# Per-chunk tiles for the scan scores and the products within a chunk

## What is computed

```python
    q_dec = q * jnp.exp(cum)
    k_inv = k * jnp.exp(-cum)
    k_end = k * jnp.exp(tot - cum)
    lower = jnp.tril(jnp.ones((HG_CHUNK, HG_CHUNK), dtype=bool))
    att = jnp.where(lower, jnp.einsum('bcthk,bcshk->bchts', q_dec, k_inv), 0.0)
    o_intra = jnp.einsum('bchts,bcshv->bcthv', att, v)
    ds = jnp.einsum('bcshk,bcshv->bchkv', k_end, v)
    ...
    o_inter = jnp.einsum('bcthk,bchkv->bcthv', q_dec, jnp.moveaxis(s_prev, 0, 1))
    return (o_intra + o_inter).reshape(b, n, h, -1), s_fin
```

## Time and profile before

| | |
|---|---|
| Time, median of 3 runs | 3948.75 us (3945.76 to 3953.18) |
| The profiled execution: its time, its span | 3950.17 us, 3948.4 us |
| Busy in the span: PE, weight loads, DVE | 2936.2, 1318.3, 2782.2 us |
| Busy in the span: ACT, POOL | 676.8, 1314.6 us |
| Mean granted clock of TensorE | 0.875 of full speed |

### The profile page before, as it was taken

The page is one execution under the profiler, slowest core; times in us unless marked ns, Lnnn a source line. Parts: engine busy times, 40 slices in busy tenths (PEclk is TensorE's granted clock), DMA queues, the critical chain, the costliest instruction groups (busy, mean ns, idle before and its releaser), DMA issues.

```text
span 3948.4 us, 46329 instructions
## 1 busy us (share of the span) xinstructions
PE 2936.2 (74%) x16906; PEld 1318.3 (33%) x16906; DVE 2782.2 (70%) x6805; ACT 676.8 (17%) x1391; POOL 1314.6 (33%) x1174
## 2 busy tenths in 40 slices
PE   8999999988899997856666666656656666665555
PEld 3665665545444442212222222212212222221111
DVE  4545546766787786747888868877877886877555
ACT  2534533011122120000111110110111111101000
POOL 0000000013433443433444434444444444444443
PEclk9999999989999998978888778878877788887777
DMA  4010003579999999999999999999999999999998
GB/s 184 24 35 26 24 25 150 183 259 404 410 414 417 412 399 417 416 422 414 400 399 413 418 409 411 417 414 415 418 413 412 419 412 416 416 411 413 420 419 340
DMA packets 214904, 1346.40 MB, mean 341 GB/s; under 512 B 24818, under 2 KB 45810, under 8 KB 63762
## 3 DMA queue, kind: packets, MB, share of 16 engines
q0 software_dynamic: 165888, 1208.03, 74.4%
q1 hardware_dynamic: 47492, 132.79, 9.0%
q10 hardware_dynamic: 1296, 2.62, 0.2%
HBM read 1329.69 MB, written 13.67 MB: 340 GB/s over the span
## 4 chain that ended last, share of the span: by engine, by line
DMA 37%; PE 36%; DVE 13%; issue 10%; POOL 2%; ACT 1%; POOLq 0%; SPq 0%; DVEq 0%; ACTq 0%
DMA arena<-in_uv,mask_b 14%; PE ps L787 12%; DMA arena<-in_uv,mask_f 11%; DMA arena<-in_uv,ones 11%; PE ps L1465 10%; DVE arena L1306 4%; PE ps L652 3%; PE ps L765 3%; POOL arena L621 2%; DVE arena L1187 2%; PE ps L1459 2%; PE ps L683 1%; PE ps L716 1%; DVE arena L1147 1%; PE ps L1517 1%
## 5 line engine op out<-in xcount | busy, mean ns | idle before, releaser
L787 PE MATMUL ps<-arena 64*64 64x512 f32 x9216 | 1451.0, 756 | 952.6 <-DVE arena L1187 946.9
L1306 DVE CUSTOM_DVE_ANT_0 arena<-arena 128x1024 f32<-128x1024 f32 x1152 | 1411.1, 1225 | 740.7 <-DMA arena<-in_uv,mask_b 292.9
L787 PEld LDWEIGHTS ps<-arena 64*64 64x64 f32 x9216 | 349.8, 157 | 1896.4 <-DVE arena L1187 1389.2
L621 POOL DMA_INDIRECT arena<-in_uv,ones x384 | 440.7, 1148 | 622.6 <-PE ps L787 480.8
L621 POOL DMA_INDIRECT arena<-in_uv,mask_f x384 | 441.3, 1149 | 584.9 <-PE ps L787 495.6
L621 POOL DMA_INDIRECT arena<-in_uv,mask_b x384 | 426.9, 1112 | 593.4 <-PE ps L787 506.4
L982 ACT ACTIVATE arena<-arena 128x2 f32<-128x2 f32 x576 | 117.1, 203 | 2646.1 <-DVE arena L1306 2645.8
L1465 PE MATMUL ps<-arena 128*128 128x384 f32 x1152 | 384.3, 490 | 1.8 <-DVE arena L1752 1.8
L1187 DVE TENSOR_SCALAR arena<-arena 128x64 f32<-128x64 f32 x1152 | 307.9, 310 | 0.4 <-ACT arena L982 0.3
L765 PE MATMUL ps<-arena 128*128 128x384 f32 x768 | 268.3, 496 | 0.0
L603 POOL IOTA arena<- 128x16 f32 x1 | 0.1, 144 | 804.0 <-PE ps L665 804.0
(11 more groups left out here) (209 smaller groups left out, 2358.6 us busy)
## 6 DMA issues: line engine op xcount, KB each, us to landing
arena<-in_w_mg SPq DMA_DIRECT2D x16, 1536.0 KB, 21.4
arena<-in_w_in SPq DMA_DIRECT2D x28, 512.0 KB, 3.4
arena<-in_w_mod SPq DMA_DIRECT2D x8, 1792.0 KB
arena<-in_w_mod SPq DMA_DIRECT2D x4, 2048.0 KB, 23.4
arena<-in_w_out SPq DMA_DIRECT2D x2, 4096.0 KB, 16.9
arena<-in_w_q SPq DMA_DIRECT2D x8, 1024.0 KB, 16.2
arena<-in_w_q SPq DMA_DIRECT2D x4, 2048.0 KB, 35.9
arena<-x_scratch SPq DMA_DIRECT2D x15, 512.0 KB, 11.6
```

The costliest lines, as they stand in the source:

```text
L621: nc.gpsimd.indirect_dma_start(out=RG[n % RING], out_offset=None, in_=uv, in_offset=bass.IndirectOffsetOnAxis(ap=EIDX[t % 3][:, s:s + 1], ...
L787: mm = nc.tensor.matmul(PS[c * HALF:(c + 1) * HALF, 2 * r + n, :], DG[rows, s, :], RG[s][rows, D + n * 512:D + (n + 1) * 512], start=(g == ...
L1306: ins = v.tensor_tensor_reduce(u, u, h2, 1.0, 0.0, ALU.mult, ALU.add, PRE[:, s % RING:s % RING + 1])
```

## The change

In `scores`, the one matmul of scores becomes four, one for each chunk: 32 columns of weights and 32 moving columns, each into its own 32 rows of the same 32 columns of bank 2. The copy by ACT has 160 columns in place of 256, the masked copy by DVE 32 in place of 128, under a mask `mask_c` that eight small copies build at the start of the heads' part. In `outputs`, the one matmul within the chunks becomes four on the array's diagonal, 32 rows and 32 columns of weights, each with the 128 value columns of its own 32 rows.

```diff
+    mask_c = sb("mask_chunk", [P, 2, CHUNK])
...
                 nc.tensor.transpose(PS[:, 2, 0:P], KE[d][:, sl], ident[:])
-                nc.tensor.matmul(PS[:, 2, P:2 * P], KI[d][:, sl], QD[d][:, sl],
-                                 start=True, stop=True).then_inc(ket_r, 1)
+                for j in range(CPT):
+                    c = slice(tt * P + j * CHUNK, tt * P + (j + 1) * CHUNK)
+                    mm = nc.tensor.matmul(PS[j * CHUNK:(j + 1) * CHUNK, 2, P:P + CHUNK], KI[d][:, c], QD[d][:, c],
+                                          start=True, stop=True)
+                mm.then_inc(ket_r, 1)
...
-                nc.tensor.matmul(OUT, ATT[:, d, it % 2, :], Vt[:, tt, :], start=True, stop=False)
+                for j in range(CPT):
+                    own = slice(j * CHUNK, (j + 1) * CHUNK)
+                    nc.tensor.matmul(OUT[own], ATT[own, d, it % 2, 0:CHUNK], Vt[own, tt, :], start=True, stop=False)
...
-                A(KET[:, it % 2, :], PS[:, 2, 0:2 * P], ACT.Copy).then_inc(ket_e, 1)
+                A(KET[:, it % 2, 0:P + CHUNK], PS[:, 2, 0:P + CHUNK], ACT.Copy).then_inc(ket_e, 1)
...
         dve.wait_ge(s_c, 2)
+        for d, m in enumerate((mask_f, mask_b)):
+            for j in range(CPT):
+                own = slice(j * CHUNK, (j + 1) * CHUNK)
+                ins = v.tensor_copy(mask_c[own, d, :], m[own, own])
+        ch(ins)
 
         v.memset(ef[:], 0.0).then_inc(lru_done, 1)
...
-                v.copy_predicated(ATT[:, d, it % 2, :], (mask_f, mask_b)[d][:].bitcast(I32),
-                                  KET[:, it % 2, P:2 * P]).then_inc(att_m, 1)
+                v.copy_predicated(ATT[:, d, it % 2, 0:CHUNK], mask_c[:, d, :].bitcast(I32),
+                                  KET[:, it % 2, P:P + CHUNK]).then_inc(att_m, 1)
```

## The result

The changed kernel takes 3962.3 us (median, 3956.72 to 3965.11) against 3948.18 for the kernel before, both over 9 runs: ratio 1.0033, 95% interval 1.0025 to 1.0042. It is slower by 14 us, where 3961 was forecast. The profiled execution took 3962.74 us, its span is 3961.0 against 3948.4.

The account below looks back on a forecast made before the run. PE was taken to bound the head-by-head part, DMA the rest. Over four heads, 3.66 us lost in projection steps less 0.48 gained elsewhere gave +12.7 us, so 3961 us against the median 3948.75; range 3951 to 3971.

Parts of the forecast that it names:

- What bounds: Head-by-head part: PE is the bound, and what the scan gains or loses arrives at the end at full size.
- The price list: On PE: tile change 0.09 us, exposed load 0.11 (128 columns) or 0.03 (32), pass 0.11 or 0.03, four tiles 0.02.
- Scores in a projection step: Scores as four tiles in steps with a projection: 0.40 us for 0.22, +0.18, between +0.12 and +0.34.
- Products in a projection step: Products within a chunk as four 32*32 tiles, steps with a projection: 0.36 us for 0.22, +0.14.
- The lower bound: Products: change from 32*32 to 128*32 is free, +0.02 us a projection step, +4.1 in all, 3953; 12%.
- Gate steps: Steps 0 to 5 of each head: the outputs' products get cheaper, -0.06 us a step.
- What was costed at nothing: Narrower ACT and DVE copies and eight mask copies (at most 2.3 us): hidden, except ACT's copy ahead of step 0.
- Off the chain from step 1 on: ACT's copies: in the chain of waits only ahead of a head's step 0, where the shorter copy saves 0.08 us.
- The sum: Four heads, each 3.66 us lost in projection steps and 0.48 gained elsewhere: +12.7 us, 0.3% slower.
- Free changes around the new tiles: Rival: tile changes that no row shows cost nothing and loads run ahead; 10.4 us faster, 3938; 5%.
- Turns of the four diagonal tiles: Rival: the products' four 32*32 tiles run in turns, +0.66 us in all 72 steps, +47, about 4009; 3%.
- The clock: Rival: PE's granted clock falls to 1.2 GHz in the gate steps, 21 us more, about 3982; 4%.

Follow-up runs that it names:

- e1: Kernel before with only the products within a chunk as four 32*32 tiles, scores and both copies unchanged: 3952.57 us, ratio 1.0014.
- e2: Kernel before with only the scores as four 128*32 tiles, both copies at old width, products unchanged: 3955.1 us, ratio 1.0024.
- e4: Kernel before with 48 extra matmuls of 128*128 tile and 128 moving columns inside late projection halves: 3958.74 us, ratio 1.0031.
- e12: Kernel before with late scores behind the outputs' 128*32 tiles, DVE's second-mixer piece first, 32*32 products in gate steps only: 3943.34 us, ratio 0.9987.
- e5: Kernel before with scores of steps 7 to 17 as 128*32 tiles behind the previous step's outputs, DVE copying from bank 7: 3980.76 us, ratio 1.008.
- e3: Kernel before with 48 extra matmuls of 128*32 tile and 128 moving columns inside late projection halves: 3975.67 us, ratio 1.0074.
- e7: The changed kernel itself, run again for comparison with reordered versions: 3961.88 us, ratio 1.0036 against the kernel before.
- e11: The changed kernel itself, run once more to look at its granted clock: 3964.11 us in one run.

## Why the prediction was right, point by point

**What bounds.** Right: the 0.30 us by which each projection step grew on PE is in the time, and L653 starts 12.0 us later. Nothing behind it took the shift up, and the experiments say the same: in e1, e2, e4 and e12 L652 starts 4.5, 7.1 and 11.1 us later and 5.0 earlier than before, and the medians differ from before by 4.5, 7.0, 10.7 and -4.9 us. In the other runs the two agree within about 2 us as well, but for e5, where L652 starts 35.0 us later and the median is 31 us higher.

**The price list.** Right to 0.02 us. It was read from the distances between starts around existing groups, and it held for two kinds of tile that no row had shown. e3 and e4 measured its main item by itself: 0.31 us for two changes with their exposed loads, where the list gives 0.09 + 0.03 + 0.09 + 0.11 = 0.32. How the sum splits into changes and loads is read from starts (above), not varied in a run.

**Scores in a projection step.** +0.18 forecast, +0.17 measured in e2. The doubt was whether passes of 32 columns are cheaper; the group takes 0.20 us where one with 128 columns takes 0.36, so they are.

**Products in a projection step.** +0.14 forecast, +0.13 in e1. The lower bound, a free change from 32*32 to 128*32, falls: load to load takes 0.35 us. "TensorEngine Tiling (Array Packing)" of the Trainium skill, Key Properties, makes no exception for any pair, and the trace agrees for these as well.

**Gate steps.** -0.06 forecast, -0.04 to -0.05 measured. The direction was right; a group of four that starts after a wait takes 0.38 us from load to load and not 0.35 as in the late steps, which the list had not.

**What was costed at nothing.** ACT's and DVE's narrower copies left no trace in the steps of 3.12 us: e1 with full copies has the same. Ahead of a head's first step, where the engines go one after the other, ACT's copy stands in the chain with 0.31 us in place of 0.39, the 0.08 of the forecast. "Off the chain from step 1 on" was not quite so: the copy for step 1 stands in it as well (0.38 us at 138.35 before, 0.30 at 138.09 after), worth another 0.08 us a head, 0.3 in all. The mask copies took 1.5 us inside the wait, under the bound of 2.3.

**The sum.** +12.7 forecast; +12.0 at L653, +12.6 in the span, +14.1 between the medians, whose interval, 1.0025 to 1.0042, is 10 to 17 us. From the steps, a head loses 11 x 0.30 + 0.13 = 3.43 us with projections, where 3.66 was forecast, and gains 0.39 with gates and at its start, where 0.48 was: 4 x (3.43 - 0.39) = 12.2. The two errors partly cancel, which is luck, though each is small. What the medians hold beyond the scans' 12 isn't settled. The interval covers it, the part from L652 or L653 to the end takes 3292.9 to 3299.2 us over the fourteen profiles, and the clock's falls of e7 and e11 cost 1.6 and 3.9 us; but e7's profiled execution, with its fall, took 3958.95 us, less than the 3962.74 of the one without.

**The rivals.** Free changes around the new tiles: falls by the rows above. Turns of the four diagonal tiles: falls, 0.35 us for the eight records. With 32*32 tiles, too, four groups of rows write one PSUM bank side by side, in rows (partitions) of their own, eight records in 0.35 us where turns would take eight passes of 0.11. "TensorEngine Tiling (Array Packing)" of the Trainium skill, Gotcha 1, read as forbidding that, doesn't fit this case. The clock: I gave it 4% as a fall through all gate steps, worth 21 us. It exists in a small form instead, in some heads of some executions, and why only there stays open.

## What to carry to other kernels

Splitting a matmul into tiles of the wanted blocks saves passes, but each change of the array's tile costs about 0.1 us and lays the next weight load open, and that cost shows on the line of the next matmul: count changes of shape along PE's order, not matmuls or columns. Put small tiles next to others of the same shape, or where PE waits anyway. And before moving a result later, look at what stands behind its reader in that engine's queue: here the same 128*32 scores made a kernel of 3981 or of 3945 us, by the order of two calls on DVE.

## What the runs showed of the hardware

A change of tile shape on PE cost 0.09 to 0.10 us of emptying for each pair seen (worked out from starts and loads), 32*32 to 128*32 and 128*32 to 128*128 among them, and a load of 128 columns of weights behind it another 0.10 us. Four 128*32 tiles with 32 moving columns took 0.20 us with that emptying, and only 0.06 behind a group of the same shape. The granted clock can fall to 1.2 GHz within a scan whose PE is never idle for long: in e7 it did so from 441.5 to 448.3 us, after PE had been busy in 14.12 of the 15 us from 425 to 440 and idle for 0.58 us at most at a time.
